# Seven half-size block products for eight in three projections of an mLSTM, mixture-of-experts decoder step

## The reference

```python
h = _rmsnorm(x, norm_mix_g)
z = jnp.einsum('btd,dc->btc', h, w_in).astype(f32)
q, k, v, o = (z[..., i * W:(i + 1) * W] for i in range(4))     # W = 512
...
u = z[..., g0 + 2 * H:]                                         # 512 columns
h_a, C, n, m = _mlstm(heads(q) * DH ** -0.5, heads(k), heads(v), ...)
h_b, buf = _pool_mixer(u, buf0.astype(f32), start_pos, w_pool, pool_scale)
x = x + jnp.einsum('btc,cd->btd', mix, w_out)
y = _moe(_rmsnorm(x, norm_ffn_g).reshape(B * T, -1), ...)       # 64 experts, top 8, and a shared one
x = x + y
```

## Time and profile before

| | us |
|---|---|
| median of 3 runs | 1015.6 |
| lowest and highest | 1012.25 and 1019.2 |
| span of the profiled execution | 1012.6 |
| TensorE busy in it | 956.0 (94%) |
| VectorE busy | 425.3 (42%) |
| GpSimd busy | 347.6 (34%) |
| ScalarE busy | 147.3 (15%) |

### The profile page before, as it was taken

The page is one execution under the profiler, slowest core; times in us unless marked ns, Lnnn a source line. Parts: engine busy times, 40 slices in busy tenths (PEclk is TensorE's granted clock), DMA queues, the critical chain, the costliest instruction groups (busy, mean ns, idle before and its releaser), DMA issues.

```text
span 1012.6 us, 16171 instructions
## 1 busy us (share of the span) xinstructions
PE 956.0 (94%) x5994; PEld 418.5 (41%) x5994; DVE 425.3 (42%) x1218; ACT 147.3 (15%) x360; POOL 347.6 (34%) x444
## 2 busy tenths in 40 slices
PE   7999999999999899999999987979998999989996
PEld 5777655665554333233222332323232222333442
DVE  4311222345568534443344434233433343432885
ACT  4000023411022111000001100001000010103232
POOL 7000321310145544453444444334434344440132
PEclk9999999999999999999999998989998999999999
DMA  9033214222179799999999999999999999988932
GB/s 284 3 94 105 83 64 131 84 73 84 39 250 381 295 340 408 413 409 410 414 412 412 414 413 413 406 391 402 413 405 398 374 413 410 412 316 346 422 133 84
DMA packets 76115, 297.50 MB, mean 294 GB/s; under 512 B 15622, under 2 KB 26062, under 8 KB 49149
## 3 DMA queue, kind: packets, MB, share of 16 engines
q1 hardware_dynamic: 60133, 258.68, 65.5%
q0 software_dynamic: 15904, 37.79, 9.7%
HBM read 276.56 MB, written 31.50 MB: 304 GB/s over the span
## 4 chain that ended last, share of the span: by engine, by line
PE 65%; DMA 23%; issue 4%; DVE 4%; POOL 2%; SPq 1%; DVEq 1%; ACT 0%; POOLq 0%; ACTq 0%
PE bank L1991 22%; PE bank L2334 18%; DMA arena<-in_ex_w 9%; PE bank L2329 8%; DMA arena<-xs_dram,slot 6%; PE bank L2429 5%; DMA ring<-in_ex_w 5%; PE bank L2174 2%; PE bank L1997 2%; POOL arena L992 2%; DMA arena<-y_dram 1%; DMA ring<-in_w_in 1%; PE bank L2098 1%; PE bank L2088 1%; PE bank L2138 1%
## 5 line engine op out<-in xcount | busy, mean ns | idle before, releaser
L2334 PE MATMUL bank<-arena 128*32 128x512 f32 x1440 | 269.4, 605 | 9.9 <-issue 5.2
L992 POOL DMA_INDIRECT arena<-xs_dram,slot x192 | 207.6, 1081 | 69.4 <-issue 57.7
L2334 PE MATMUL bank<-ring,arena 128*32 128x512 f32 x864 | 212.6, 606 | 5.2 <-DMA arena<-in_ex_w 5.1
L1008 POOL DMA_INDIRECT y_dram<-arena,outrow x46 | 47.1, 1024 | 269.2 <-DVE slot L1751 217.1
L2334 PE MATMUL bank<-xT,arena 128*32 128x512 f32 x576 | 114.7, 604 | 5.3 <-DMA ring<-in_ex_w 5.3
L2334 PEld LDWEIGHTS bank<-arena 128*32 128x32 f32 x1440 | 67.3, 111 | 110.9 <-issue 103.8
L1765 DVE STREAM_TRANSPOSE arena<-arena 128x1024 f32<-128x1024 f32 x48 | 59.7, 1244 | 88.7 <-DMA arena<-xs_dram,slot 88.5
L1991 PE MATMUL bank<-xT,ring 128*128 128x288 f32 x384 | 93.4, 406 | 0.8 <-DMA ring<-in_w_in 0.8
L2334 PE MATMUL bank<-mixpj,arena 128*32 128x512 f32 x384 | 84.7, 594 | 0.0
L1991 PEld LDWEIGHTS bank<-xT,ring 128*128 128x128 f32 x384 | 72.9, 190 | 21.0 <-DMA ring<-in_w_in 1.0
L2334 PEld LDWEIGHTS bank<-ring,arena 128*32 128x32 f32 x864 | 50.9, 111 | 49.7 <-issue 43.6
(11 more groups left out here) (421 smaller groups left out, 1239.7 us busy)
## 6 DMA issues: line engine op xcount, KB each, us to landing
arena<-in_ex_w SPq DMA_DIRECT2D x78, 1024.0 KB, 21.9
ring<-in_ex_w SPq DMA_DIRECT2D x50, 1024.0 KB, 26.8
xT<-in_ex_w SPq DMA_DIRECT2D x28, 1024.0 KB
mixpj<-in_ex_w SPq DMA_DIRECT2D x24, 1024.0 KB, 20.2
arena<-y_dram SPq DMA_DIRECT2D x18, 1024.0 KB, 11.0
wide<-in_ex_w SPq DMA_DIRECT2D x12, 1024.0 KB, 25.6
ring<-in_w_in SPq DMA_DIRECT2D x5, 2048.0 KB, 8.3
ring<-in_w_out SPq DMA_DIRECT2D x2, 2048.0 KB, 8.6
```

Of the source, the lines that this page charges most:

```text
L992: pool.indirect_dma_start(xg[b][:, 256 * a:256 * a + 256], None, xs_quarter, bass.IndirectOffsetOnAxis(slot[k][:, a:a + 1], 0), bounds_che ...
L1008: pool.indirect_dma_start(y_dram, bass.IndirectOffsetOnAxis(outrow[b][:, 0:1], 0), og[b], None, bounds_check=K * T - 1, oob_is_err=False). ...
L2334: ins = pe.matmul(b[t, :], lhs[:, t], rhs(home(own if lane < 3 else common)), start=start, stop=stop)
```

## The change

q, k and u are each computed as a product of 2x2 blocks: output features in two halves of 256 (each two tiles m of 128), tokens in two halves of 288, features summed over in two halves of four chunks. In place of eight block products there are seven, by Winograd's form of Strassen's scheme, each with two PSUM groups (m = 0 and 1) of four matmuls 128x128 by 128x288. The operands of four of them are sums: S1 to S4 of weight blocks (128 x 1024 elements each, made for each of q, k, u) and T1, T2, T3, N4 of blocks of xT (128 x 1152 elements each, made once), all on VectorE. The results are put together from the products: ScalarE copies product 1 out of its banks (keep), VectorE adds products 2, 6, 7, 5, 3, 4 to running sums in SBUF (14 additions of 128x288 a chunk, added and the loop in blocks) and multiplies the four finished blocks by the token factor as before (8 times, finished and scaled; three instructions for u where they touch the samples).

On SP q's load stands right behind x, in two halves with a semaphore each (s_qhalf for the first), k's right behind it, and the two loads of wg and their wait for s_const come after these, with the small loads. On TensorE the gate product comes behind q, and the second piece of rB inside q. On VectorE the first part of the gate chain stands behind q's blocks, the scans behind k's and the copy and halving of rstd (L1365 to L1368) behind u's. The sums S1 to S3 of the next chunk are made between product 5 and product 3 of the chunk before, S4 behind product 3. GpSimd's memset of ones in v moves from the start to behind buf, ahead of its first window sum.

```diff
-    g += [(("rB", 0), "s"), (("g",), "v"), (("rB", 1), "s")]
-    g += [(("q", j, n), "v") for j in range(H) for n in range(2)]
-    g += [(("k", j, n), "v") for j in range(H) for n in range(2)]
-    g += [(("u", j, n), "v") for j in range(H) for n in range(2)]
+    g += [(("rB", 0), "s")]
+    for name in ("q", "k", "u"):
+        g += [((name, 1, m), "s") for m in range(2)] + [((name, 2, m), "v") for m in range(2)]
+        if name == "q":
+            g += [(("rB", 1), "s")]
+        g += [((name, n, m), "v") for n in (6, 7, 5, 3, 4) for m in range(2)]
+        if name == "q":
+            g += [(("g",), "v")]
...
+        S1, S2 = (v_raw[:, 1024 * k:1024 * k + 1024].rearrange("p (c n) -> p c n", c=4) for k in range(2))
+        S3, S4 = (pool_raw[:, H * EXT + 1024 * k:H * EXT + 1024 * k + 1024].rearrange("p (c n) -> p c n", c=4)
+                  for k in range(2))
+        T1, T2, T3, N4 = (mixpj[:, 4 * TH * k:4 * TH * (k + 1)].rearrange("p (c t) -> p c t", t=TH) for k in range(4))
+        kept = [[so_raw[:, NT * P + TH * (2 * b + m):NT * P + TH * (2 * b + m + 1)] for m in range(2)] for b in range(2)]
+        blk = [junk[:, TH * m:TH * m + TH] for m in range(2)]
...
-            sp.wait_ge(s_const, 1)
-            sp.dma_start(wg[:, :, 0:H], wi[:, :, 4 * MW:4 * MW + H]).then_inc(s_wg, 16)
-            sp.dma_start(wg[:, :, 32:32 + H], wi[:, :, 4 * MW + H:4 * MW + 2 * H]).then_inc(s_wg, 16)
...
-            load_chunk("q")
+            wq = chunk("q").rearrange("p (c n) -> p c n", n=512)
+            sp.dma_start(wq[:, 0:4], wi[:, 0:4, 0:512]).then_inc(s_qhalf, 16)
+            sp.dma_start(wq[:, 4:8], wi[:, 4:8, 0:512]).then_inc(s_ring[0], 16)
+            load_chunk("k")
+            sp.wait_ge(s_const, 1)
+            sp.dma_start(wg[:, :, 0:H], wi[:, :, 4 * MW:4 * MW + H]).then_inc(s_wg, 16)
+            sp.dma_start(wg[:, :, 32:32 + H], wi[:, :, 4 * MW + H:4 * MW + 2 * H]).then_inc(s_wg, 16)
...
-            load_chunk("k")
...
+                    pool.memset(v[:, :, :, P:DE], 1.0).then_inc(s_ones, 1)
...
+            def keep(name):
+                k = PROJ.index(name)
+                for m in range(2):
+                    b = full_bank(act, name, 1, m)
+                    if k >= 2:
+                        wait_drained(act, PROJ[k - 2], 3, m)
+                    drain("s", act.copy(kept[k % 2][m], b[:, 0:TH]), name, 1, m)
+            spread(0, 0, SEQ)
+            keep("q")
+            spread(1, SEQ, T)
+            keep("k")
             act.wait_ge(s_abs, 1)
             act.activation(r_e, r_e, ACT.Exp, scale=-1.0).then_inc(act_step, 1)
             act.wait_ge(act_step, 1)
             act.activation(r_l, r_e, ACT.Ln, bias=1.0).then_inc(s_ln, 1)
+            keep("u")
...
+            x11, x12 = xT[:, 0:4, 0:TH], xT[:, 0:4, TH:T]
+            x21, x22 = xT[:, 4:8, 0:TH], xT[:, 4:8, TH:T]
+            wait_drained(dve, "x1T", NT - 1, 1)
+            summing(dve.tensor_tensor(T1, x12, x11, ALU.subtract), "q", "T1")
+            dve.wait_ge(s_qhalf, 16)
+            chunk_in(dve, "q")
+            sum1("q")
+            dve.wait_ge(s_sum, SUM_AT["q", "T1"])
+            summing(dve.tensor_tensor(T2, x22, T1, ALU.subtract), "q", "T2")
+            sum2("q")
+            summing(dve.tensor_tensor(T3, x22, x12, ALU.subtract), "q", "T3")
+            sum3("q")
+            sum4("q")
+            dve.wait_ge(s_sum, SUM_AT["q", "T2"])
+            summing(dve.tensor_tensor(N4, x21, T2, ALU.subtract), "q", "N4")
+            dve.wait_ge(s_sq, NT)
+            wait_drained(dve, "rB", 0)
...
+            def added(name, n, outs, ins_):
+                at = []
+                for m in range(2):
+                    b = full_bank(dve, name, n, m)
+                    at.append(mark(dve.tensor_tensor(outs[m], b[:, 0:TH], ins_[m], ALU.add)))
+                return at
+            def finished(name, n, row, col, srcs, at):
+                for m in range(2):
+                    dve.wait_ge(dve_step, at[m])
+                    ins = scaled(name, 2 * row + m, col, srcs[m])
+                    drain("v", ins, name, n, m)
+            def blocks(name, after_name):
+                top = kept[PROJ.index(name) % 2]
+                for m in range(2):
+                    wait_drained(dve, name, 1, m)
+                at = added(name, 2, blk, top)
+                finished(name, 2, 0, 0, blk, at)
+                if name == "q":
+                    wait_drained(dve, "rB", 1)
+                for n, into in ((6, top), (7, low)):
+                    for m in range(2):
+                        b = full_bank(dve, name, n, m)
+                        if n == 7:
+                            wait_drained(dve, name, 6, m)
+                        drain("v", dve.tensor_tensor(into[m], b[:, 0:TH], top[m], ALU.add), name, n, m)
+                wait_drained(dve, name, 7, 1)
+                at = added(name, 5, blk, low)
+                most = added(name, 5, top, top)
+                finished(name, 5, 1, 1, blk, at)
+                if after_name:
+                    chunk_in(dve, after_name)
+                    sum1(after_name)
+                    sum2(after_name)
+                    sum3(after_name)
+                dve.wait_ge(dve_step, most[1])
+                at = added(name, 3, top, top)
+                finished(name, 3, 0, 1, top, at)
+                if after_name:
+                    sum4(after_name)
+                at = added(name, 4, low, low)
+                finished(name, 4, 1, 0, low, at)
+            blocks("q", "k")
...
+            blocks("k", "u")
             dve.wait_ge(s_ln, 1)
             link(dve.scalar_tensor_tensor(out=r_l, in0=r_f, scalar=0.0, in1=r_l, op0=ALU.min, op1=ALU.subtract))
...
+            blocks("u", None)
+            dve.wait_ge(s_rstd, NT)
...
+            def seven_products(name):
+                w = chunk(name).rearrange("p (c n) -> p c n", n=512)
+                x11, x12 = xT[:, 0:4, 0:TH], xT[:, 0:4, TH:T]
+                x21, x22 = xT[:, 4:8, 0:TH], xT[:, 4:8, TH:T]
+                w11, w12, w22 = w[:, 0:4, 0:256], w[:, 4:8, 0:256], w[:, 4:8, 256:512]
+                def product(n, lhs, rhs):
+                    for m in range(2):
+                        b = free_bank(pe, name, n, m)
+                        reduce_over(b[:, 0:TH], lambda c: lhs[:, c, P * m:P * m + P], lambda c: rhs[:, c, :], 4
+                                    ).then_inc(filled, 1)
+                if name == "q":
+                    pe.wait_ge(s_qhalf, 16)
+                    wait_drained(pe, "x1T", 2, 0)
+                else:
+                    chunk_in(pe, name)
+                product(1, w11, x11)
+                if name == "q":
+                    chunk_in(pe, name)
+                    wait_drained(pe, "x1T", 2, 1)
+                product(2, w12, x21)
+                if name == "q":
+                    spread_rstd(1, (NP_,))
+                pe.wait_ge(s_sum, SUM_AT[name, "S2"])
+                product(6, S2, T2)
+                pe.wait_ge(s_sum, SUM_AT[name, "S3"])
+                product(7, S3, T3)
+                product(5, S1, T1)
+                pe.wait_ge(s_sum, SUM_AT[name, "S4"])
+                product(3, S4, x22)
+                pe.wait_ge(s_sum, SUM_AT["q", "N4"])
+                product(4, w22, N4)
             spread_rstd(0, range(NP_))
-            wait_drained(pe, "x1T", NT - 1, 0)
-            wait_drained(pe, "x1T", NT - 1, 1)
+            seven_products("q")
             pe.wait_ge(s_wg, 32)
             b = free_bank(pe, "g")
             for c in range(KT):
@@ -2027,15 +2194,8 @@
                     ins = pe.matmul(b[NS * n:NS * n + 36, 0:TH], wg[:, c, :], xT[:, c, TH * n:TH * n + TH],
                                     start=(c == 0), stop=(c == KT - 1))
             ins.then_inc(filled, 1)
-            spread_rstd(1, (NP_,))
-            for name in ("q", "k", "u"):
-                chunk_in(pe, name)
-                w = chunk(name).rearrange("p (c n) -> p c n", n=512)
-                for j in range(H):
-                    for n in range(2):
-                        b = free_bank(pe, name, j, n)
-                        reduce_over(b[:, 0:TH], lambda c: w[:, c, P * j:P * j + P],
-                                    lambda c: xT[:, c, TH * n:TH * n + TH], KT).then_inc(filled, 1)
+            seven_products("k")
+            seven_products("u")
```

More of the change, by code:

```diff
@@ L312, in decoder_step @@
         nout = over(c_at + MW + H * NS + P, 2 * P)[0:NB * H, :]
-        ppo = mx(MW)[0:R, :]
-        pso = mx(MW)[0:NS, :]
+        pp_raw, pp_at = carve("mixer", 2 * MW)
+        ppo = pp_raw[0:R, 0:MW]
+        pso = pp_raw[0:NS, MW:2 * MW]
+        low = [pp_raw[:, TH * m:TH * m + TH] for m in range(2)]
         fac = mx(6 * NT * H).rearrange("p (k i h) -> p k i h", i=NT, h=H)
@@ L821, in _ @@
             pool.memset(reset[:, SEQ:T:DS], NEG)
-            pool.memset(v[:, :, :, P:DE], 1.0)
             pool.memset(uext[:, :, 0:R], 0.0)
```

(24 more changed lines are left out.)

66 lines of the change are left out of this document (41 added, 25 removed).

## The result

The change makes the kernel 1.1% faster: median 1004.8 us (1002.89 to 1005.88) against 1016.5 us of the kernel before on the same chip, ratio 0.9892 (95% interval 0.9870 to 0.9913), so 11.6 us less where 12.5 were forecast; 1003.1 was predicted, and 1004.8 lies in the likeliest case's own range of 999 to 1008. Two further comparisons of the same kernel gave 0.9905 (0.9879 to 0.9930) and 0.9902 (0.9884 to 0.9919): 9.6 and 10.7 us. The three together say 10.6 us, and 12.5 us (1.2%) lies just outside the intervals of the last two, so the forecast was some 2 us too high. The profiled execution has a span of 1001.1 us for 1012.6.

What follows compares the result with a forecast made beforehand. TensorE's unbroken chain through q, k and u was taken to bound the stage, its end passing to the load-bound expert loop. -11.64 - 0.84 = -12.5 us off the 1015.6 median gave 1003.1 us, whole range 998 to 1010.

Steps and rivals of the forecast that it cites:

- likeliest case: The gain comes through, 12.5 us off to 1003.1 us; chance 72%, own range 999 to 1008 us.
- Removed matmuls: In q, k and u, 56 matmuls a chunk for 64, at 0.485 us each: 11.64 us less.
- Group starts: 42 PSUM groups for 24 in q, k and u cost 0 beyond their matmuls; upper bound 0.7 to 1.7 us.
- The start: The wait for q's weights goes, saving 0.84 us, first product at 12.7; lower bound a loss of 1.8 us.
- The sums: VectorE's block sums delay nothing, value 0, with 2.0 us of slack at product 6; bound 1.8 us, once.
- VectorE's load: Additions, scalings and sums take VectorE 15.0 us a chunk against 27.2 us of TensorE, so no waits.
- Behind u: VectorE starts window sums about 2.0 us later; absorbed with 0.8 us left, otherwise about 1 us lost.
- The loop: The expert loop's loads start on TensorE's chain, so the loop moves with it and the gain is kept.
- Losses at the start or in the sums: Rival, 15%: late q half, late sums, group starts or pooling leave 5.5 to 9 us won, 1006.5 to 1010.
- The loop that swallows it: Rival, 8%: expert loads at 0.99 of the time end when they end, so the time is 1015 us.
- VectorE that cannot follow: Rival, 3%: VectorE too slow per chunk makes TensorE wait by the banks; at 35 us a chunk 1027 us.
- The clock through bank changes: Rival, 2%: bank changes each 1.94 us make TensorE's clock fall in the stage; up to 1085 us.

Runs made afterwards that it cites:

- GpSimd later: The changed kernel with GpSimd's constants held back until VectorE has made q's last sum; 1006.99 us, ratio 0.9914 to the kernel before.
- filled VectorE: The changed kernel with five idle VectorE instructions of 128x512 behind each product's additions, six times a chunk; 1034.7 us in a single execution.
- order alone: The kernel before with q's weights and product ahead of the gate product, still eight products; 1015.64 us, ratio 1.0003.
- seven eighths: The kernel before with the last 128 features left out of q, k and u: 56 matmuls a chunk, no sums or additions; 1006.88 us, ratio 0.9909.
- delayed changed kernel: The changed kernel with 25 idle matmuls (12.1 us) on TensorE behind u; 1016.50 us, ratio 1.0012 to the kernel before.
- delayed kernel before: The kernel before with 13 idle matmuls (6.3 us) on TensorE behind u; 1021.58 us, ratio 1.0060.

## Why the prediction was right, point by point

**Removed matmuls: right.** 11.64 us were forecast; with the start left as it was the stage became 93.42 - 81.78 = 11.64 us shorter. Group starts: 0 of a possible 0.7 to 1.7, right, since 56 matmuls in 14 groups and in 8 take the same 81.78. The spacing of 0.485 taken from VectorE's emptyings was good to 0.002.

**The start: a size that isn't constant.** Forecast 0.84 saved, first product at 12.7 to 13.0. The first trace came near (12.62), but the other two of the changed kernel came at 13.16 and 14.72, with waits of 0.29 and 0.61 for q's first half. Taken over the three traces of the changed kernel and the two of before, u's end moved by 11.77 us, not 12.34, so of the 0.84 some 0.1 is left. Over all traces it is 0.3: with the start of before the first product comes at 18.74 on average (five traces) and 81.78 us of seven products follow, with the new start at 13.74 (eight traces) and 86.50 follow. The step that failed is the 0.84 taken from one execution, where a wait ends with transfers whose hour scatters by 2 us. The forecast had a lower bound for this term, but for another reason, that wg did not slow q; the scatter itself was not in it, and that the first trace gave 12.34 was luck. That wg's pieces held up q was right in direction: in front of q they had held SP's q issue for 3.84 us; ahead of them q's two halves took 0.58 and 0.63, k's 0.92, and they themselves 5.80 and 5.29. The forecast had 2.6 for the two, and "4 us of standstill"; it was 11.1, and the small loads were issued by 24.6 all the same, so nothing was late.

**The sums: right by their slack, wrong in one price.** VectorE, from the start of the sums (rows with start, us, form and the wait before):

```profile
12.53 1.36 DVE L1402 TENSOR_TENSOR mixpj<-xT 128x1152 f32<-128x1152 f32 x1
15.33 1.23 DVE L1383 TENSOR_TENSOR arena<-ring 128x1024 f32<-128x1024 f32 x1 [1.45 <-DMA ring<-in_w_in]
17.75 1.31 DVE L1388 TENSOR_TENSOR arena<-arena,ring 128x1024 f32<-128x1024 f32 x1
```

S2 ended at 19.06 (forecast 19.0), and product 6 started at 20.89 (21.0): 1.8 us of slack. For GpSimd's hindrance the value 0 was taken from one small instruction, L1341; but S3 took 1.66 where it takes 1.22 without GpSimd. The right price was +0.8 over eight sums and only 0.1 of it by S2, where the bound was 3.8. The step that failed is the transfer of a price: L1341 is 576 elements on four partitions, and that it met no hindrance in its 0.75 us was read as a rule for eight instructions nearly twice as long. The same rows had a hint on the other engine: beside L1341 GpSimd's selection of 128x4 (L860) took 0.51 us, where the same instruction took 0.19 in the run with GpSimd later. The Trainium skill (GPSIMD Engine Reference, 1. Specifications) had the two engines in contention where VectorE has two SBUF inputs; the runs agree, with these 0.8 us, and with 4.6 us on five of GpSimd's own instructions (L844 to L856, 6.37 us in the changed kernel for 1.77 in the kernel before).

**VectorE's load: right.** It was busy 55.63 of 86.50 us, and only the two tests that doubled its sums or nearly doubled its load brought waits, in the places named: product 6, and the banks.

**Behind u: right.** The first window sum of GpSimd started 2.8 us behind u's end (101.91), where it was 1.5: 1.3 us later for the 2.0 forecast, and the third sum was still no hold-up:

```profile
108.60 4.25 POOL L904 TENSOR_TENSOR arena<-arena 128x710 f32<-128x710 f32 x3 [1.22 <-DVE arena L1548]
114.32 0.68 DVE L1539 SCALAR_TENSOR_TENSOR arena<-arena 128x496 f32<-128x496 f32 x1 [0.29 <-PE bank L2225]
```

VectorE, on its way to use the next sums, waited 0.29 for TensorE, not for GpSimd. From u's end to the first expert load it is 179.2 us in every trace, but for the filled VectorE and the two with a delay in between.

**The loop: right.** Not swallowed: delays come out one for one, and so did the gain. From the load until the rows are there the three traces of the changed kernel have 649.0 us on average, the two of before 650.0; all traces together go from 648.6 to 653.2, so this 1.0 is within the scatter.

**The tail: not foreseen.** The forecast let everything behind the stage keep its length. The second tile's rows were waited for 15.6 to 15.9 us in all traces with fewer matmuls (15.54 with the filled VectorE), 14.7 to 14.9 in those of the kernel before and of the order alone. The wait begins earlier, so that costs little by itself. But TensorE's idle time before it went from 1.44 to between 2.13 and 2.60, and the clock then fell in seven of nine traces: rest 73.3 to 74.1 instead of 72.3. So -11.8 at u's end, -1.0 in the loop, +1.7 in the rest make -11.1; the mean of the spans moved by 11.0 (1002.3 and 1013.3). What was missing in the forecast is a term of up to 1.7 us for TensorE's clock behind the stage, and a question about the idle stretches that the kernel already had. This term and the 0.6 to 0.7 us of the start are the two that make the forecast some 2 us too high.

What stays open is why the second tile's rows come back 1 us later behind the first's: from TensorE's taking up the first tile's last rows it is 9.9 us in the kernel before and with the order alone, 11.0 in the changed kernel, 11.1 with seven eighths and 10.8 in the delayed changed kernel. It isn't the seven products (the seven eighths have 15.94), nor the order (14.68), nor the hour (15.66 in the delayed changed kernel, 14.93 in the delayed kernel before). What those with 15.5 or more share is 24 matmuls less in the projections; no run here ties the two. That the fall of the clock comes from this longer idleness fits the traces, but with two of nine against it, it is not shown.

**The rivals.** Losses at the start or in the sums: at the start 0.6 to 0.7 us of the 0.84, in the sums nothing, together far from half the gain. The loop that swallows it fell with the delays. VectorE that cannot follow is real: the filled one, at 34 us a chunk, was slower than the kernel before by 20 us in its one execution. For 35 us a chunk the forecast had 11, because it counted the three chunks alone and not the 13 us that the filled kernel loses behind them; but the changed kernel, with 55.63 of 86.50 us, is far from it. The clock through bank changes fell: 1.00 in a stage with a bank change each 1.94 us. The Trainium skill (TensorE: Matmul & The Clock Gate, A second HAM failure mode: psum-queue depth-cycling) describes swings where banks are gone round; the trace doesn't show them here, where groups follow each other without a pause.

## What to carry to other kernels

Where one engine runs without a break and hands its end on to whatever comes next, work taken from it can be worth its full time (here 11.6 us at the end of the stage), and extra work on an engine that is idle half the time is free as long as each deadline has its own slack; find the tightest one (here 1.8 us for the second sum) and test it by doubling its cause. Don't take a wait at a transfer's arrival from one execution: the 0.84 us of this case was smaller than the scatter of the arrival, 2 us. And look behind the stage for idle stretches of the engine whose clock can fall; a gain of 12 us went with a loss of up to 1.7 in one of them, and a wait of 2.5 us in the stage cost 4.2.

## What the runs showed of the hardware

- The clock in the tail: 1.00 after 1.43 to 1.45 us idle (four traces, 24 records in 10.54 us), and after 2.1 to 2.6 us lowered in seven of nine (up to 12.23 us). In the stage, 2.49 us idle gave 0.53 over the next 3 us. With six matmuls in the stretch, idle 0.84 behind them, it stayed (one trace).
- Two loads of 16 KB in 16-byte pieces held SP's queue for 5.80 and 5.29 us with 4 MB of weights queued ahead of them (5.71 to 6.84 and 5.29 in the eight traces with this start); the issue of the last 2 MB of those took 0.92. Behind x alone the same two took 0.58 and 2.04.
- A sum of two SBUF inputs, 128x1024 in float32, took 1.22 us alone and up to 1.66 beside GpSimd's small constant-making instructions; of these, 128x128 selections went from 0.28 to 0.94 and 1.26 us beside such sums, and stayed at 0.28 beside additions with one input out of PSUM. Memsets kept their length beside such sums.
- 128x128 by 128x288 in float32 takes 0.485 to 0.487 us whether 4, 7 or 8 of them make a PSUM group.
